# Taking the last 128 tokens out of the dense expert products

## What is computed

```
s = einsum(q, subkeys); sv, si = top_k(s, 16)              # per head, two halves of 128 keys
top_s, pos = top_k(sv[0][:, None] + sv[1][None, :], 16)    # 16 of 256 pairs
experts = si[0] * 128 + si[1] at pos;  gates = softmax(top_s)
hid = gelu(einsum('nkd,nd->nk', u_table[experts], x)) * gates      # 128 a token
y   = einsum('nk,nkd->nd', hid, v_table[experts])
```

## Time and profile before

| | |
|---|---|
| times of three runs | 3446.53, 3447.34 and 3449.43 us; median 3447.34 |
| the profiled execution, span | 3448.0 us |
| busy: PE, weight load, DVE, ACT, POOL | 3410.4, 2809.0, 2085.6, 1157.1, 736.6 us |
| mean granted TensorE clock | 0.997 of 2.4 GHz |
| HBM read, written | 364.22 MB, 69.21 MB |

### The profile page before, as it was taken

How to read it: one execution, slowest core, us unless ns; L and a number is a source line. 1 busy time by engine, 2 the same in 40 slices (tenths; PEclk the granted TensorE clock), 3 DMA queues, 4 the chain that set the end, 5 groups by cost and what they waited for, 6 DMA issues and landing times.

```text
span 3448.0 us, 45451 instructions
## 1 busy us (share of the span) xinstructions
PE 3410.4 (99%) x17112; PEld 2809.0 (81%) x17112; DVE 2085.6 (60%) x3178; ACT 1157.1 (34%) x1573; POOL 736.6 (21%) x299
## 2 busy tenths in 40 slices
PE   8999999999999999999999999999999999999999
PEld 7688888888888888888888888888888777778887
DVE  6686199998888835555555667454444534445573
ACT  4452343344444421111111332233332435423322
POOL 2303344300000034444444300010000342132000
PEclk9999999999999999999999999999999999999999
DMA  5111345456556664444444233233332221122322
GB/s 171 57 44 57 97 127 144 145 161 186 183 179 188 186 250 193 190 190 190 190 190 190 91 98 98 90 100 97 96 95 96 95 86 44 41 70 92 97 90 94
DMA packets 145538, 437.41 MB, mean 127 GB/s; under 512 B 12288, under 2 KB 47488, under 8 KB 136960
## 3 DMA queue, kind: packets, MB, share of 16 engines
q1 hardware_dynamic: 144448, 432.95, 37.6%
q10 hardware_dynamic: 960, 2.65, 0.3%
HBM read 364.22 MB, written 69.21 MB: 126 GB/s over the span
## 4 chain that ended last, share of the span: by engine, by line
PE 45%; issue 41%; POOL 10%; DVE 1%; ACT 1%; DMA 1%; POOLq 0%; SPq 0%; DVEq 0%; ACTq 0%
PE ring_banks L273 13%; PE ring_banks L275 13%; PE ring_banks L274 13%; POOL vlo L884 6%; POOL wlo L871 4%; PE ring_banks L1538 1%; PE work_banks L1507 1%; PE work_banks L1510 1%; DMA slot<-w 1%; PE work_banks L1525 0%; PE work_banks L273 0%; PE work_banks L274 0%; PE work_banks L275 0%; ACT whi L1650 0%; DVE newt L2338 0%
## 5 line engine op out<-in xcount | busy, mean ns | idle before, releaser
L273 PE MATMUL ring_banks<-xx,wlo 128*128 128x512 f32 (+1 forms) x2704 | 1057.0, 391 | 3.5 <-POOL wlo L871 1.3
L275 PE MATMUL ring_banks<-xx,whi 128*128 128x512 f32 (+1 forms) x2704 | 1047.3, 387 | 0.0
L274 PE MATMUL ring_banks<-xx,whi 128*128 128x512 f32 (+1 forms) x2256 | 875.2, 388 | 0.0
L1650 ACT ACTIVATE whi<-slot 128x1024 fp32r<-128x1024 f32 x427 | 451.6, 1060 | 996.2 <-DMA slot<-w 570.0
L871 POOL TENSOR_TENSOR wlo<-slot,whi 128x1024 fp32r<-128x1024 f32 x163 | 407.5, 2506 | 1391.3 <-ACT whi L1650 1391.0
L275 PEld LDWEIGHTS ring_banks<-xx,whi 128*128 128x128 f32 x2704 | 508.3, 188 | 105.1
L273 PEld LDWEIGHTS ring_banks<-xx,wlo 128*128 128x128 f32 x2704 | 508.7, 188 | 104.5 <-ACT av L1835 1.4
L884 POOL TENSOR_TENSOR vlo<-v,vhi 128x1024 fp32r<-128x1024 f32 x128 | 322.0, 2545 | 921.2 <-ACT vhi L2022 921.2
L274 PEld LDWEIGHTS ring_banks<-xx,whi 128*128 128x128 f32 x2256 | 424.4, 188 | 84.6 <-issue 0.2
L2218 DVE TENSOR_TENSOR wlo<-slot,whi 128x1024 fp32r<-128x1024 f32 x264 | 321.4, 1223 | 152.6 <-ACT whi L1650 142.7
L2022 ACT ACTIVATE vhi<-v 128x1024 fp32r<-128x1024 f32 x128 | 125.0, 1048 | 549.1 <-DMA v<-v 541.0
(11 more groups left out here) (479 smaller groups left out, 4819.7 us busy)
## 6 DMA issues: line engine op xcount, KB each, us to landing
slot<-w SPq DMA_DIRECT2D x301, 512.0 KB, 3.5
slot<-u SPq DMA_DIRECT2D x128, 512.0 KB, 4.0
v<-v SPq DMA_DIRECT2D x32, 2048.0 KB, 11.6
early<-early SPq DMA_DIRECT2D x128, 256.0 KB, 4.1
ge<-early SPq DMA_DIRECT2D x32, 1024.0 KB, 7.3
gates<-stage SPq DMA_DIRECT2D x63, 512.0 KB, 5.1
gbuf<-gates SPq DMA_DIRECT2D x31, 1024.0 KB, 4.8
hT<-xT SPq DMA_DIRECT2D x8, 256.0 KB, 6.7
```

What stands on the lines that cost most here:

```text
L273: pe.matmul(out, w[1], x[0], start=start, stop=False)
L274: pe.matmul(out, w[0], x[1], start=False, stop=False)
L275: return pe.matmul(out, w[0], x[0], start=False, stop=stop)
L1650: act.activation(whi[s % RING], slot[s % RING], ACT.Copy).then_inc(whr, 1)
```

## The change

`T` = 512 tokens become `TD` = 384 in the dense expert products, the early values and the gates; ranking stays for all 512, and the last 128 tokens (one on each partition) are ranked first.

- Ranking the last tile gives row numbers (`number_rows`) and gates, which stay on the tokens' partitions. Its normed activations are transposed by PE (16 products with the identity) and copied to `xt` by ACT.
- POOL issues an indirect transfer for each of the 128 choices, from a row-major table of U, and later of V: 128 rows of 4 KB, one for each partition. DVE multiplies a U row by `xt` and sums it to one number (`use_u`), and adds a V row, weighted, to one of two sums (`use_v`). 96 U rows stand in the one-hot steps, two a step, 16 beside the last tiles, 16 in the first four groups; V rows in 26 of the groups.
- The rows' buffers lie where `hT` and `xn` were: SP writes `hT` to HBM before the stage and loads it again in group 6.
- Ahead tiles are 10 for each token tile (40), 13 for every 64 tokens (78 in 48 steps), and the last ten. All their slabs are subtracted by POOL, in a written order with the indirect transfers.
- In the groups V is loaded in quarters, gates and early values into three buffers. POOL subtracts three V slabs of four, DVE the fourth (`v_low`); the cast to `ghi` goes from DVE to ACT (`weight_high`). POOL starts on V after the last tile.
- The last group transposes the sum of the rows into columns 384 to 511 of each bank.

```diff
+GT = TT - 1
+TD = GT * P
-AHEAD = 11
-PER_STAGE = 10
+AHEAD = 10
+PER_STAGE = 13
@@ order of the rows
+ROW_STEPS = TD // BATCH
+ROWS_IN_TAIL, ROWS_FIRST = 16, 4
+U_RING, V_RING = 4, 6
+    at_step = [[2 * x, 2 * x + 1] for x in range(ROW_STEPS)]
+    tail = list(range(2 * ROW_STEPS, 2 * ROW_STEPS + ROWS_IN_TAIL))
+    rest = list(range(2 * ROW_STEPS + ROWS_IN_TAIL, SLOTS))
+    u_at = {g: rest[ROWS_FIRST * g:ROWS_FIRST * g + ROWS_FIRST] for g in range(len(rest) // ROWS_FIRST)}
+    first = len(u_at) + 1
+    count = GROUPS - 1 - first
+    v_at = {first + g: list(range(SLOTS * g // count, SLOTS * (g + 1) // count)) for g in range(count)}
@@ gpsimd
+            def fetch_u(s):
+                if s >= U_RING:
+                    pool.wait_ge(r_use, s - U_RING + 1)
+                pool.indirect_dma_start(u_row[s % U_RING], None, a["u_rows"],
+                                        bass.IndirectOffsetOnAxis(ap=row_at[:, s:s + 1], axis=0)).then_inc(r_l[s % U_RING], 16)
-            split_slabs(U_AT, AHEAD * TT)
-            with pool.Fori(0, 16) as i:
-                for b in range(2):
-                    split_v(b, i)
+            split_slabs(U_AT, 16)
+            pool.wait_ge(r_ix, 1)
+            pool.wait_ge(r_kept, 16)
+            for s in range(U_RING):
+                fetch_u(s)
+            u = 16
+            for x in range(ROW_STEPS):
+                until = AHEAD * TT + 2 * (x + 1) * PER_STAGE // 16 + 3
+                while u < until:
+                    split_slab(U_AT + u)
+                    u += 1
+                for s in U_ROWS_AT_STEP[x]:
+                    fetch_u(s + U_RING)
+            for s in U_ROWS_IN_TAIL:
+                if u < KEYS:
+                    split_slab(U_AT + u)
+                    u += 1
+                fetch_u(s + U_RING)
+            pool.wait_ge(done, TILE_AT["hid"] + KEYS)
+            for g in range(GROUPS):
...
+                for r in range(3):
+                    split_v(g, r)
+                    for fetch, s in rows[2 * r:2 * r + 2] if r < 2 else rows[4:]:
+                        fetch(s)
@@ tensor
-                    mm = product(pe, bank, pick(slab(U_AT + u), k), pick((xh, xlo), k, slice(0, T)), k == 0, k == 7)
+                    mm = product(pe, bank[:, 0:TD], pick(slab(U_AT + u), k), pick((xh, xlo), k, slice(0, TD)), k == 0, k == 7)
@@ vector
+            def use_u(s):
+                row = u_row[s % U_RING]
+                dve.wait_ge(r_l[s % U_RING], 16 * (s // U_RING + 1))
...
+                dve.scalar_tensor_tensor(row, row, 1.0, xt, ALU.mult, ALU.mult, accum_out=row_hid[:, s:s + 1]).then_inc(r_use, 1)
+            def use_v(s):
...
+                dve.scalar_tensor_tensor(total, row, row_w[:, s:s + 1], total, ALU.mult, ALU.add).then_inc(r_use, 1)
@@ vector, one-hots
-                    while low < (x + 1) * 2 * PER_STAGE * BATCH // (2 * STAGE):
-                        slab_low(U_AT + AHEAD * TT + 2 * PER_STAGE * (t0 // (2 * STAGE)) + low, i, 2 * PER_STAGE)
-                        low += 1
+                    for s in U_ROWS_AT_STEP[x]:
+                        use_u(s)
@@ vector, groups
+            for g in range(GROUPS):
+                apply_gates(g)
+                rows = [(use_u, s) for s in U_ROWS_AT.get(g, ())] + [(use_v, s) for s in V_ROWS_AT.get(g, ())]
...
+                for use, s in rows[0:2]:
+                    use(s)
+                weight_low(g)
+                v_low(g)
+                for use, s in rows[2:]:
+                    use(s)
```

More of the change, by code:

```diff
@@ L101, in _low_counts @@
             by_vector = (who and not (name in ("pin0", "cin", "pin1") and slab < start + 7) or
-                         name == "ri" and slab == start + 3 or
-                         name == "u" and slab >= U_AT + AHEAD * TT)
+                         name == "ri" and slab == start + 3)
             n[by_vector] += 1
@@ L812, in _ @@
             sp.dma_start(a["gates"][1:4, :, last].rearrange("g i n -> i g n"),
[L813 to L827, removed]
+                         stage[last % 2][:, 1:4].rearrange("p g r t -> p g (r t)")).then_inc(p_gw[1], 16)
             write_gates(last, 1, p_gw[1])
@@ L1342, in _ @@
                     mm.then_inc(done, 1)
+            for k in range(KD):
+                o = psB[:, 2 + k // 4, k % 4 * P:(k % 4 + 1) * P]
+                pe.matmul(o, xh[:, k, TD:T].bitcast(F32), ident, start=True, stop=False)
+                mm = pe.matmul(o, xlo[:, k, TD:T].bitcast(F32), ident, start=False, stop=True)
+            mm.then_inc(p_tp, 1)
             def ahead_tile(u, i=None, per=4):
@@ L1397, in spread @@
                     for d in range(KD):
-                        mm = product(pe, out_bank(d), pick((vhi[b], vlo[b]), r, slice(d * P, (d + 1) * P)),
-                                     (ghi[b][:, :, r, :], glo[b][:, r, :]), first and r == 0, False)
-                mm.then_inc(p_y, 1)
+                        mm = product(pe, out_bank(d)[:, 0:TD], pick((vhi[b], vlo[b]), r, slice(d * P, (d + 1) * P)),
+                                     (ghi[c][:, :, r, :], glo[c][:, r, :]), first and r == 0, False)
@@ L1402, in spread_last @@
+                    mm.then_inc(p_y, 1)
             def spread_last(g):
-                b = g % 2
+                b, c = g % 2, g % 3
+                pe.wait_ge(p_w, 4 * g + 4)
+                pe.wait_ge(p_vs, 3 * g + 3)
+                pe.wait_ge(p_vd, g + 1)
                 for d in range(KD):
                     for r in range(4):
[L1406 to L1411, removed]
@@ L1413, in _ @@
-            pe.wait_ge(p_st, T // 4)
-            pe.wait_ge(out_, TILE_AT["hid"] + KEYS)
[L1415 to L1421, removed]
+                        product(pe, out_bank(d)[:, 0:TD], pick((vhi[b], vlo[b]), r, slice(d * P, (d + 1) * P)),
+                                (ghi[c][:, :, r, :], glo[c][:, r, :]), False, r == 3)
@@ L1424, in pool_layer @@
+                    if d == 0:
+                        pe.wait_ge(r_use, 2 * SLOTS + 1)
+                    pe.transpose(out_bank(d)[:, TD:T], y_sum[0][:, d * P:(d + 1) * P], ident).then_inc(p_yd, 1)
+            pe.wait_ge(p_st, TD // 4)
+            pe.wait_ge(out_, TILE_AT["hid"] + KEYS)
+            spread(0, first=True)
+            with pe.Fori(0, 5) as i:
+                for g in range(1, 7):
+                    spread(g, i)
+            spread_last(GROUPS - 1)
             def pool_layer(j):
@@ L2025, in _ @@
+            act.wait_ge(p_om, TD // 4)
             for u in range(KEYS - TAIL, KEYS):
@@ L2762, in gated @@
-                    step.wait()
-                    step(dve.tensor_copy(ghi[b][:, :, r, :], weight))
-                    step.wait()
-                    dve.tensor_tensor(glo[b][:, r, :].rearrange("p (t n) -> p t n", n=STAGE), weight,
-                                      ghi[b][:, :, r, :].bitcast(F32), ALU.subtract).then_inc(p_w, 1)
-            step(dve.memset(wfwf[:, :, 0:1], 1.0))
-            step(dve.tensor_tensor(wfwf[:, :, 1], pcol("fin1", 0, KD), pcol("fin1", 0, KD), ALU.mult))
-            with dve.Fori(0, 16) as i:
-                step.enter(i, 16)
-                for b in range(2):
-                    gated(b, i)
-                step.leave(16)
+                    dve.tensor_tensor(weight, weight, gbuf[b][:, :, r, :], ALU.mult).then_inc(p_gm, 1)
@@ new lines, in weight_low, with v_low @@
+            def weight_low(g):
+                b = g % 3
+                for r in range(4):
+                    dve.wait_ge(p_gh, 4 * g + r + 1)
+                    dve.tensor_tensor(glo[b][:, r, :].rearrange("p (t n) -> p t n", n=STAGE),
+                                      ge[b][:, r, :].rearrange("p (t n) -> p t n", n=STAGE),
+                                      ghi[b][:, :, r, :].bitcast(F32), ALU.subtract).then_inc(p_w, 1)
+            def v_low(g):
+                b = g % 2
+                dve.wait_ge(p_vh, 4 * g + 4)
+                dve.tensor_tensor(vlo[b][:, 3, :], vbuf[b][:, 3, :], vhi[b][:, 3, :].bitcast(F32), ALU.subtract).then_inc(p_vd, 1)
```

341 lines of the change are left out of this document (216 added, 125 removed).

## The result

The changed kernel takes 3420.6 us (median of 4 runs, 3417.1 to 3423.9) against 3446.9 for the kernel before on the same chip: a ratio of 0.9923, 95% interval 0.9911 to 0.9936. I forecast 3391: faster it is and inside the range, but it gained 26 us where I had 57. The ratios compare executions of the usual speed: two of e9's six, at 12.8 and 15.5 ms, are left out and not explained.

What follows compares the result with a forecast made beforehand. PE, 99% busy, was taken to bound the kernel, with DVE nearly full in A and B. Terms -14 (A), +42 (B), +23 (C), +2 and -110 (D) sum to -57 from 3448.0: 3391 us, range 3260 to 3510.

Steps and rivals of the forecast that it cites:

- C: Last tiles before the expert groups, ten instead of four: 44 us from PE work and DVE/POOL turns, +23 us.
- +2: Just after the last tile: POOL's first V subtraction, 2.4 us, stands alone before PE, adding 2 us.
- they run three tiles ahead of PE (12.5 us), so this reaches nobody: POOL's slabs waiting behind gathers: their lead over PE was to hide the wait, at no cost.
- B: Stage of one-hots and 78 tiles: 48 steps of 12.1 us, DVE taking turns with POOL's subtractions, +42 us.
- D: The 32 groups of V products: narrower products, 18.2 us in each of 26 groups, 590 us in all, -110 us.
- A: Expert tiles while DVE ranks the experts: DVE's waits for the exponential on ACT go, -14 us.
- R1: Rival: DVE and POOL take no turns in the one-hot stage and V groups; 3178 us, chance 0.13.
- My floor of 17.1 for transfers: V groups: 6.26 MB at 367 GB/s at most take 17.1 us per group.
- R3: Rival: scattered rows cost transfers one and a half times their bytes, group 20.6 us; 3453 us, chance 0.10.
- the 0.6: V groups: 0.6 us added per group because two limits, 17.6 and 17.1 us, lay close, giving 18.2.
- R2: Rival: gathers fill POOL; 3500 us at 2.55 us each, 3697 if making descriptors also takes turns; chance 0.19.
- R4: Rival: in the one-hot stage PE's clock stays at its lower level, step 16.7 us; 3612 us, chance 0.04.

Runs made afterwards that it cites:

- e9: e7 with ACT's four copies of V(0) one tile later, its eight rows kept in the last tiles; 3259.1 us, ratio 0.9455.
- e10: e7 with no U rows in the last tiles and ACT's copies of V(0) one tile later; 3254.4 us, ratio 0.9442.
- e3: Changed kernel with U slab loads first on SP's queue and eight instead of sixteen U rows in the last tiles; 3405.3 us, ratio 0.9876.
- e7: e3 and e4 together, plus all V subtractions on DVE; 3260.7 us, ratio 0.9463.
- e4: Changed kernel with U slabs from the 41st on subtracted by DVE instead of POOL; 3322.1 us, ratio 0.9635.
- e5: Changed kernel with all four V subtractions of each expert group on DVE, POOL only fetching rows there; 3374.2 us, ratio 0.9791.

## Why the prediction came out as it did

**The step that failed** is C: "Ten tiles instead of four, 41.7 us of PE; DVE and POOL in turns 16 x 1.3 + 10 x 2.27 = 43.5. I take 44: +23." With the +2 behind it that is 46; measured were 89. The price of a tile holds: e10 does eleven in 45.8 us, 4.16 each. That C has eleven, not ten, is 4 of the 43 that are missing; some 35 are PE at rest, 39 us where my 46 left 4. What fails is that the step took only PE and the sum of the turns as limits, as if the tiles' operands were there. I had followed none of SP's queue there, though the change more than doubled the tiles that stand behind the preparation of group 0, and nothing on DVE and POOL behind the rows: the +2 took POOL's first V subtraction to stand alone behind the last tile, and it stood behind gathers, 16 us later. By the runs, of the 39 us that lie between 50.1 and 89.1, the slabs' order together with eight rows less accounts for 26 (e3), the turns for some 5 (e3 to e7), the last eight rows and the V copies for 9 (e7 to e10). The shares depend on the order of removal (the turns alone were worth 10, in e4), and how much of the rows' share is the order on DVE and POOL and how much their transfers stays open. It is the same oversight as in "they run three tiles ahead of PE (12.5 us), so this reaches nobody": POOL can't run ahead of a slab that isn't loaded.

**Luck**: B came 15 shorter and D 5, which hid 20 of C's 43. Without them the gain would have been some 6 us.

**A, -14: right.** The stage ends at 662.2, and the waits for the exponential are gone from DVE's list.

**B, +42: right in mechanism, 15 too long.** A step lasted 566 / 48 = 11.8 instead of 12.1. My sum for DVE's own part was too large: by e4 it is (474.2 - 79 x 1.14) / 48 = 8.0, seven instructions 1.14 apart, and not 8.4. That bf16 instructions with two SBUF inputs take turns with POOL, for which no row of before stood, is shown by a pair of timelines (POOL, then DVE) at the same time:

```profile
1212.67 2.56 POOL L915 TENSOR_TENSOR wlo<-slot,whi 128x1024 fp32r<-128x1024 f32 x1
```

```profile
1212.91 3.40 DVE L2870 TENSOR_TENSOR oneJ<-iota,places 128x1024 bf16<-128x1024 bf16 x1
1216.24 1.21 DVE L2871 TENSOR_TENSOR hits<-iota,places 128x1024 bf16<-128x1024 bf16 x1
```

oneJ takes 3.40 beside a subtraction, where it takes 1.22 alone. R1 falls; e4's 474 comes without POOL's subtractions and is not R1's 418. My condition of two SBUF inputs said more than the earlier trace rows, where a CAST with one was held up as well. DVE also waited 10.6 us for gathers, which I had at nothing.

**D, -110: right in size**, with -115 in the windows, and in its main cause. Products start 0.173 us apart, as the timeline of PE shows against the earlier trace rows:

```profile
1499.76 0.33 PE L295 MATMUL ring_banks<-ghi,vlo 128*128 128x384 f32 x1
1499.94 0.33 PE L296 MATMUL ring_banks<-glo,vhi 128*128 128x384 f32 x1
```

The mean of the 26 groups with V rows was 18.2, though not evenly: about half take 16.6, the others 17 to 23. e5 shows that the turns, not the transfers, made the difference. My floor of 17.1 for transfers was wrong: with V rows in every group, 16.6 are held at 407 GB/s in e10, so the 363 of the earlier trace rows, on which the floor and R3 rest, was no limit. First the changed kernel, 1440 to 1880, then e10:

```profile
1440.00:1880.00 440.00, 415.04 (x2309) 411.09 (x2308) 440.00 (x332) 143.72 (x193) 361.37 (x185) 0.97 0.92 336
1400.00:1700.00 300.00, 300.00 (x1733) 300.00 (x1732) 280.59 (x325) 107.30 (x145) 163.66 (x105) 1.00 1.02 407
```

DVE never rests in the first, so its own sum was 18.2 and not 17.6, and the 0.6 that I added because of the transfers came out right by luck.

**R2** fails by its price: groups of gathers on POOL, 662 to 1228 in the changed kernel and 662 to 1140 in e4, then two of the changed kernel's in the tail, with DVE at rest.

```profile
L935 POOL DMA_INDIRECT u_row<-u_rows,row_numbers x94 | 157.8, 1679 | 21.4 <-issue 18.2
```

```profile
L936 POOL DMA_INDIRECT u_row<-u_rows,row_numbers x96 | 174.5, 1818 | 329.2 <-DVE u_row L2842 314.5 <-issue 14.6
```

```profile
1239.69 0.95 POOL L935 DMA_INDIRECT u_row<-u_rows,row_numbers  x1 [0.15 <-issue]
1240.95 0.94 POOL L935 DMA_INDIRECT u_row<-u_rows,row_numbers  x1 [0.30 <-issue]
```

0.95 us with DVE at rest, 1.7 to 1.8 beside it, around the 1.2 that I took and under the 1.9 at which POOL would have set a group. In e4 it costs DVE nothing. The Trainium skill (SBUF — State Buffer, Who interferes with whom) infers that descriptor generation stays outside the turns with a two-input DVE instruction; for DVE's side e4 agrees, its instructions staying at 1.22, for POOL's side 1.82 against 0.95 does not. The same section warns that such a transfer can be starved by DVE; POOL's side would fit that, but no run shows the port as its cause.

**R4**: the clock did fall in stretches of A, B and C (mean granted 0.90, 0.89, 0.81), where PE idles; A and B were DVE's, so it cost nothing visible there. In C it did cost: behind the first gap, 14.9 us of rest, slab 122's tile ran at a mean of 0.60, partly at the lower level of 1.2 GHz, and took 6.9 us instead of 4.2.

```profile
1263.90:1270.80 6.90, 6.90 (x25) 6.90 (x26) 1.32 (x2) 2.99 (x5) 5.00 (x3) 0.60 0.75 225
```

C's 267 products took 49.8 us of PE, e10's 264 took 45.8 at 1.00, so some 3.5 of C's 43 are the clock's, a sum that I had at nothing.

## What to carry to other kernels

Where a change lengthens a loop, list for each in-order queue what stands between its iterations and what comes behind: six slab loads behind a block that used to have none behind it left PE idle for 15 us, and sixteen rows that wait for transfers, ahead of another block on DVE and on POOL, for 21. A stage in which no engine is full is not priced by adding busy times; follow its first and last operand back through the queues. And an operation moved to an idle POOL isn't free: beside a DVE that was busy with instructions of two SBUF inputs, the 1.14 us that each saved DVE were paid back at 2.2 (e4).

## What the runs showed of the hardware

A gather's descriptors on POOL and DVE's two-input instructions interfere on one side only: the gather stretches from 0.95 to 1.8 us, DVE's instructions stay at 1.22 (e4, 96 gathers beside 476 us of busy DVE). DVE's accumulator output was an instruction of its own of 0.08 us:

```profile
1222.04 0.08 DVE L2847 DVE_READ_ACCUMULATOR u_row<-u_row,token_rows 128x1 f32 x1
```

Gathers of scattered rows of 4 KB moved with the rest at 407 GB/s over 300 us (e10), so scattering did not cost the transfers half as much again, as R3 had feared.
